# Rotary cosine product and sum moved from GpSimd to VectorE, and convolution taps ended at tile 19 of the input stage instead of 20.5

## What is computed

```python
def _apply_rope(x, cos, sin):
    re, im = xf[..., 0, :], xf[..., 1, :]
    out = jnp.stack([re * cs - im * sn, im * cs + re * sn], axis=-2)

def _conformer_conv(u, dw, dw_bias, ln_g, ln_b):
    a, g = jnp.split(u, 2, axis=-1)
    v = a * jax.nn.sigmoid(g)
    y = lax.conv_general_dilated(v, dw[:, None, :], ...) + dw_bias     # 31 taps, 384 channels
    return jax.nn.silu(_layer_norm(y, ln_g, ln_b))

# _token_mixer: proj = h @ w_in, split into
#   dk dv gk gv | u_f dq gq u_c gate_logits; rotary on dq, dk, gq, gk
```

## Time and profile before

| what | value |
|---|---|
| median of 3 runs | 3684.27 us (3684.15 to 3689.58) |
| the profiled execution's own time | 3683.18 us |
| its span | 3681.4 us |
| busy PE, DVE, ACT, POOL | 3471.7, 1915.6, 1394.8, 193.9 us |
| mean granted clock of TensorE | 0.972 of full speed |
| matmuls | 18528 |

### The profile page before, as it was taken

How to read it: one execution, slowest core, us unless ns; L and a number is a source line. 1 busy time by engine, 2 the same in 40 slices (tenths; PEclk the granted TensorE clock), 3 DMA queues, 4 the chain that set the end, 5 groups by cost and what they waited for, 6 DMA issues and landing times. The chain is left out here.

```text
span 3681.4 us, 46723 instructions
## 1 busy us (share of the span) xinstructions
PE 3471.7 (94%) x18528; PEld 2727.1 (74%) x18528; DVE 1915.6 (52%) x2940; ACT 1394.8 (38%) x2383; POOL 193.9 (5%) x126
## 2 busy tenths in 40 slices
PE   7999999989999999997999999999997999989999
PEld 5888898765777677876765677778885776767767
DVE  4655676856544434444866544454444365333653
ACT  3544443244443322224334443322223444333442
POOL 0000000310000100001220000000001000000000
PEclk8999999999999999998999999999998999989999
DMA  5555465211123643333221122223332221222112
GB/s 192 187 197 191 137 183 158 69 58 40 52 64 103 229 160 121 102 97 106 75 69 42 50 63 91 88 70 97 97 97 82 70 63 41 91 83 73 58 41 97
DMA packets 97260, 366.73 MB, mean 100 GB/s; under 512 B 11168, under 2 KB 11424, under 8 KB 95520
## 3 DMA queue, kind: packets, MB, share of 16 engines
q1 hardware_dynamic: 97056, 363.84, 31.0%
HBM read 354.36 MB, written 9.44 MB: 99 GB/s over the span
## 5 line engine op out<-in xcount | busy, mean ns | idle before, releaser
L355 DVE TENSOR_TENSOR w_lo<-w_raw,w_hi 128x1024 fp32r<-128x1024 f32 x529 | 653.9, 1236 | 609.8 <-ACT w_hi L345 609.6
L369 PE MATMUL banks<-h_hi,w_hi 128*128 128x512 f32 (+2 forms) x2040 | 807.8, 396 | 21.2 <-DVE h_lo L1026 8.5
L371 PE MATMUL banks<-h_hi,w_lo 128*128 128x512 f32 (+2 forms) x2040 | 749.7, 367 | 0.0
L370 PE MATMUL banks<-h_lo,w_hi 128*128 128x512 f32 (+2 forms) x2040 | 748.6, 367 | 0.0
L345 ACT ACTIVATE w_hi<-w_raw 128x1024 fp32r<-128x1024 f32 x545 | 573.3, 1054 | 314.6 <-DMA w_raw<-in_stream 303.5
L369 PEld LDWEIGHTS banks<-h_hi,w_hi 128*128 128x128 f32 (+1 forms) x2040 | 394.1, 193 | 124.7 <-issue 52.5
L371 PEld LDWEIGHTS banks<-h_hi,w_lo 128*128 128x128 f32 (+1 forms) x2040 | 392.8, 193 | 64.7
L370 PEld LDWEIGHTS banks<-h_lo,w_hi 128*128 128x128 f32 (+1 forms) x2040 | 394.9, 194 | 58.8 <-issue 10.6
L369 PE MATMUL banks<-merged_hi,w_hi 128*128 128x512 f32 (+1 forms) x960 | 341.0, 355 | 4.1 <-DVE mid L1457 2.3
L370 PE MATMUL banks<-merged_lo,w_hi 128*128 128x512 f32 (+1 forms) x960 | 338.2, 352 | 0.0
L371 PE MATMUL banks<-merged_hi,w_lo 128*128 128x512 f32 (+1 forms) x960 | 338.2, 352 | 0.0
(11 more groups left out here) (386 smaller groups left out, 4764.7 us busy)
## 6 DMA issues: line engine op xcount, KB each, us to landing
w_raw<-in_stream SPq DMA_DIRECT2D x545, 512.0 KB, 3.6
mod_cells<-in_stream SPq DMA_DIRECT2D x48, 512.0 KB, 5.9
mod_cell<-in_stream SPq DMA_DIRECT2D x48, 512.0 KB, 5.3
x_kept<-x SPq DMA_DIRECT2D x3, 2048.0 KB, 7.2
x<-x_kept SPq DMA_DIRECT2D x3, 2048.0 KB, 8.1
x<-in_x SPq DMA_DIRECT2D x2, 2048.0 KB, 8.7
out_x<-x SPq DMA_DIRECT2D x8, 256.0 KB, 4.3
dft_table<-in_dft SPq DMA_DIRECT2D x2, 768.0 KB, 7.3
```

The source lines that it names most:

```text
L355: (by or self.nc.vector).tensor_tensor(self.lo[:, c], self.raw[:, c], self.hi[:, c].bitcast(F32), ALU.subtract)\
L369: self.nc.tensor.matmul(out, w_hi, x_hi, start=start, stop=False)
L370: self.nc.tensor.matmul(out, w_hi, x_lo, start=False, stop=False)
L371: mm = self.nc.tensor.matmul(out, w_lo, x_hi, start=False, stop=stop)
```

## The change

Two things change. First, `AxialRope.pool` goes, and its two instructions for each tile are issued by VectorE in `AxialRope.dve`: the cosine product directly behind the sine product, the sum at a mark 0.2 tiles later. They keep their buffers and semaphores. Second, `until` of the convolution is 19.0 instead of 20.5. This applies to all three executions of the stage, with the context among them.

```diff
@@ AxialRope.dve
             nc.vector.tensor_tensor(self.b[:, n % 2], self.bank(n), self.tables[:, 1, 0:self.I.NT], ALU.mult)\
                 .then_inc(self.with_sin.sem, 1)
-
-    def pool(self, pool):
-        nc = self.I.K.nc
-        pool.wait_ge(self.table_in.sem, self.table_in.at(16))
-        for n, item in enumerate(self.items):
-            yield item[1] + 0.1
-            self.ready(pool, item)
-            nc.gpsimd.tensor_tensor(self.a[:, n % 2], item[0], self.tables[:, 0, 0:self.I.NT], ALU.mult).then_inc(self.with_cos.sem, 1)
-            yield item[1] + 0.6
-            pool.wait_ge(self.with_cos.sem, self.with_cos.at(n + 1))
-            pool.wait_ge(self.with_sin.sem, self.with_sin.at(n + 1))
-            nc.gpsimd.tensor_tensor(item[0], self.a[:, n % 2], self.b[:, n % 2], ALU.add).then_inc(self.turned.sem, 1)
+            self.ready(dve, item)
+            nc.vector.tensor_tensor(self.a[:, n % 2], item[0], self.tables[:, 0, 0:self.I.NT], ALU.mult).then_inc(self.with_cos.sem, 1)
+            yield item[1] + 0.7
+            dve.wait_ge(self.with_cos.sem, self.with_cos.at(n + 1))
+            dve.wait_ge(self.with_sin.sem, self.with_sin.at(n + 1))
+            nc.vector.tensor_tensor(item[0], self.a[:, n % 2], self.b[:, n % 2], ALU.add).then_inc(self.turned.sem, 1)
@@ input_stage
-        conv = DepthConv(inputs, glu, v, vec[:, w_at:w_at + CONV_T * CONV_K], vec[:, b_at:b_at + CONV_T], branch[:, 11:14], 20.5)
+        conv = DepthConv(inputs, glu, v, vec[:, w_at:w_at + CONV_T * CONV_K], vec[:, b_at:b_at + CONV_T], branch[:, 11:14], 19.0)
@@ input_stage, gpsimd block
-            more = [turn.pool(pool)] if turn is not None else []
-            more += [late.pool(pool)] if late is not None else []
+            more = [late.pool(pool)] if late is not None else []
```

## The result

| | before | after |
|---|---|---|
| median | 3685.78 us (3684.08 to 3693.58, 6 runs) | 3669.86 us (3662.85 to 3671.4, 6 runs) |
| ratio | | 0.9949, interval 0.9936 to 0.9962 |
| the profiled execution, its span | 3683.18, 3681.4 us | 3671.17, 3669.3 us |

The kernel became faster by 15.9 us between the medians; the ratio makes it 18.8 us, with an interval from 14.0 to 23.6. The forecast was 20.2 us and 3664 us, with a range of its own from 3660 to 3668 and a whole range from 3658 to 3675: the median lies outside the first and inside the second. A second measurement of the same program (the first experiment) gave 3666.13 us and 0.9945, inside both.

A forecast was written before the change was run, and what follows sets the result against it. TensorE, busy nearly throughout, was taken as the bound, losing time at L2459's waits and low clock. Gains of 8.6 + 8.9 + 2.7 = 20.2 us gave 3664 us; own range 3660 to 3668, whole range 3658 to 3675.

The forecast's parts named there:

- What bounds the kernel: Layer norm sum L2459 in the input stages: TensorE's wait for a late VectorE tap costs 8.6 and 8.9 us.
- Why VectorE is late: Latent input stages: each pair of GpSimd rotary instructions costs VectorE 2.05 us, nine to ten pairs missing 20 us.
- The new instructions on VectorE: Rotary tiles: 26 more per latent stage at 0.60 us each, at most 0.69; 1.2 us a tile replaces 2.05.
- The taps' end: Layer 0: the last tap ends at 731.6, or 733.3 with slower instructions, instead of 746.3; L2459's wait goes whole.
- The context: Context input stage: the tap wait becomes a shorter `w_lo` wait, 2.7 us gained, bounds 1.7 to 3.7.
- a hitch at tile 19: Context: one more TensorE delay there, with no idle time taken up, gives the lower bound of 1.7 us gained.
- TensorE back at 2.4 GHz at once: Context, behind the sums: full clock, with all idle time taken up, gives the upper bound of 3.7 us gained.
- What could be late next: Latent stages behind the last tap: later `w_lo` in time, L2496 perhaps 1.1 us late but covered by nearly 5 us.
- if the stretch behind L2459 grew by what was gained ahead of it: Sign of being wrong: TensorE's gain ahead of L2459 is lost again in the stretch behind it.
- that rival: One latent stage loses its gain or the context's `w_lo` delay costs more: 3675 us, 12 in 100.
- a part given back: Outcome with some of the gain lost, 12 in 100; the whole range, 3658 to 3675, reaches into it.
- The time: Whole kernel: 20.2 us less, a median of 3664 us; 74 in 100 for the forecast.

The follow-up runs named there:

- the first experiment: The changed kernel measured again with no edit: 3666.13 us, ratio 0.9945 to the kernel before.
- spread sums: Changed kernel with L2466's 24 one-column matmuls issued in groups of six between the next tile's blocks, later layer norm steps moved 0.75 tile: 3667.26 us, ratio 0.994.

## Why the prediction was right

**What bounds the kernel.** Right. The wait at L2459 gave what the forecast said: 8.57 and 8.89 us measured for 8.6 and 8.9, since the place behaves as built up from single matmuls (3.03 us for 3.02).

**Why VectorE is late.** Right, and shown by adding GpSimd's load back: 2.1 us a pair for 2.05. The Trainium skill (SBUF — State Buffer, Who interferes with whom) has it as an exclusive lock, when VectorE has two inputs in SBUF and GpSimd reads SBUF. That holds here in direction, but not in full: full exclusion would cost VectorE all of GpSimd's 3.35 us, and the tap and the sum together grew by 2.1.

**The new instructions on VectorE.** 0.60 each and 0.70 for a sum right behind its product; the bound was 0.69, so that a tile costs VectorE 1.2 to 1.3 us more for them. The last tap came at 731.5 for 731.6. The `w_lo` behind it was done at 728.18 + 4.5 = 732.7 for 732.8.

**The taps' end.** The forecast gave the latent stages' gain to both parts together and did not ask whether one would do. Either does, so there 19.0 brings nothing beside the rotary part. It matters where it had the smaller sum, in the context.

**The context.** The net was right, 2.68 for 2.7, but two errors cancel in it. When the stage begins, after is 1.55 us ahead of before, so 1.55 brings its rows to the clock of before. The `w_lo` of tile 20 is done at 119.47 + 1.14 + 1.55 = 122.2 (forecast 121.4), tile 20 starts at 120.84 + 1.55 = 122.4 (121.7), and the second matmul behind the sums at 125.20 + 1.55 = 126.75 (126.0). That is 2.0 us ahead of the 128.74 of before, not 2.7. The other 0.7 comes behind it: there the matmuls of before are 0.41 long, at a granted clock of 0.50 (126.9 to 130.3), and those of after 0.28, at 1.00 (126 to 130). Both stood in the step as bounds (a hitch at tile 19, and TensorE back at 2.4 GHz at once), and both came.

Where TensorE would wait was half wrong too. I said some 2 us for `w_lo` at tiles 19 and 20; it was 1.1 there, and 1.7 at a Fourier step and a head reciprocal, which stand behind more taps of VectorE than before. The step counted only `w_lo` as what the taps delay.

**What could be late next.** L2496 cost nothing, as forecast. The clock was the miss: I said that 1.00 holds across the place, and it does up to L2466, where it falls. That is 3.2 us of the 20.2 in the two latent stages, a term that the sum did not have. With it the sum is 17.0, and the five stretches measured 16.9. The forecast named "if the stretch behind L2459 grew by what was gained ahead of it" as a sign of being wrong: it grew by 1.6 of 8.6. So something was given back, by another way than that rival said. That the median still lies inside the whole range is owed to the room that the range had for a part given back, and not to the sum.

**The time.** The median is 5.9 us above the forecast's 3664. The clock behind L2466 makes 3.2 of them, and 1.5 are the kernel before itself, whose median is 3685.8 in these runs and was 3684.3 in those that the forecast started from. The last 1.2 are within what two measurements of the same program differ by (3669.9 and 3666.1).

**The rest.** The forecast put it at nothing. At each of the three losses that repeat the granted clock differs from before. In the one from 1907 to 1955 it falls at another moment. In before it is down to 0.75 from 1930 to 1935, and TensorE then waits 1.64 us for the weights of the softmax at L1599. In after it is up there, the wait is 3.24, and it falls behind the wait, where work is delayed by it:

```profile
1916.00:1921.00 5.00, 2.21 (x10) 1.50 (x8) 3.49 (x4) 3.27 (x5) 0.00 (x0) 0.95 0.00 0
1921.00:1926.00 5.00, 4.54 (x14) 2.76 (x15) 3.42 (x5) 0.93 (x3) 0.00 (x0) 0.50 0.00 0
```

At the start of the two others after has a low clock over a stretch in which TensorE has no gap, and before has 1.00 at both places (1664.2 to 1668 and 2775 to 2777.5). Half the clock over 3.4 us is about 1.7 us, by estimate: all of the loss at 2771 and most of the one at 1657.

```profile
1654.30:1657.70 3.40, 3.40 (x18) 3.40 (x18) 1.22 (x3) 2.01 (x4) 0.00 (x0) 0.50 0.00 0
...
2760.20:2763.60 3.40, 3.40 (x16) 3.40 (x17) 1.50 (x3) 2.19 (x4) 0.12 (x1) 0.50 0.03 7
```

Why a change in the input stages moves the clock so far behind them is open. In the changed kernel with the context's end at 19.75 the place from 1907 to 1955 lost nothing (0.00), with the taps alone 0.02. The 1.6 us at 2771 are in every kernel with the rotary part on VectorE but the two that have spread sums and the context's end at 19.75, and are missing with the taps alone.

## What to carry to other kernels

Look for the stretch in which two engines are both without a gap, and price a helper engine by what it takes from its neighbour: here GpSimd's seemingly free help cost VectorE 2.05 us a tile, and the same work on VectorE 1.2 to 1.3. When two edits attack one wait, ask what each would bring alone: here both brought the same 8.6 us, and their gains did not add. And when an instruction is put ahead of others on a full engine, look at every consumer behind it, not only at the one with the least slack.

## What the runs showed of the hardware

Two float32 products of 128x512 take GpSimd 3.35 us beside VectorE, and each stretches a VectorE instruction of 0.68 to 0.73 us to 1.77, also where the two share no data.

A row of 24 one-column matmuls (2.8 us, TensorE busy throughout) was followed by 1.2 GHz in after (a granted clock of 0.57 from 746.6 to 750.2) and by 2.4 GHz in before (1.00). In before TensorE had waited 6.8 us, which ended 12 us earlier, with the clock at 0.70 from 738.1 to 749.5; in after it had been busy at 1.00 for 75 us. Split into groups of six between other matmuls the same 24 left the clock at 1.00. So with the wait gone a fall of the clock came up 13 us behind the place of it, which gave back 1.6 of each 8.6 us, and 3.2 in one stage with the taps alone. It came in both latent stages of every kernel that had no wait at L2459 and the 24 in a row. That the wait itself had kept it away in before is not shown. The kernel with GpSimd busy again tells little on this: its TensorE waits 4.6 us right ahead of L2466, and the clock is down in the row itself (4.61 us long where it is 2.88 in after) and behind it (0.50 from 764 to 768), so that there the fall can belong to the wait.
